# Forget columns moved into the key-rope piece, which comes first of the feature pieces; score products on 128 rows; squares of the second block's A attention one piece ahead of their sums

## What is computed

```python
logf = jax.nn.log_sigmoid((a_f + b_forget[l]).astype(jnp.float32))   # a_f: 6 columns of h @ w_in
cum_logf = jnp.cumsum(logf, axis=1)
a_out = _fox_attention(a_q, a_k, a_v, cum_logf)       # 6 heads of 128; adds cum[q] - cum[k] to the scores
...
q_nope, q_rope = q[..., :B_NOPE], _rope(q[..., B_NOPE:], pos)
k_rope = _rope(b_krope[:, :, None, :], pos)[:, :, 0, :]              # 64 columns, the same for all heads
b_out = _mla_attention(q_nope, q_rope, k_nope, k_rope, b_v)          # 6 heads: 128 + 64 wide
...
c_out = _diff_attention(...)                                         # 4 heads, two scores of 64 each
x = x + jnp.einsum('bsm,md->bsd', mixed, w_out[l])
```

## Time and profile before

| what | value |
|---|---|
| median of 3 runs | 2325.93 us (2325.87 to 2327.4) |
| the profiled execution, its own time | 2325.4 us |
| its span, first to last instruction | 2323.6 us |
| TensorE products (PE) busy | 2164.6 us, 93% |
| VectorE (DVE) busy | 1376.7 us, 59% |
| ScalarE (ACT) busy | 727.5 us, 31% |
| DMA | 761.82 MB, mean 328 GB/s |
| mean granted clock of TensorE | 0.988 |
| the first block ends, about | 972 us |
| the second block's attention ends, about | 1340 us |

### The profile page before, as it was taken

The page is one execution under the profiler, slowest core; times in us unless marked ns, Lnnn a source line. Parts: engine busy times, 40 slices in busy tenths (PEclk is TensorE's granted clock), DMA queues, the critical chain, the costliest instruction groups (busy, mean ns, idle before and its releaser), DMA issues. The chain is left out here.

```text
span 2323.6 us, 35590 instructions
## 1 busy us (share of the span) xinstructions
PE 2164.6 (93%) x14439; PEld 1634.7 (70%) x14439; DVE 1376.7 (59%) x2161; ACT 727.5 (31%) x1317; POOL 37.3 (2%) x62
## 2 busy tenths in 40 slices
PE   7999999999999999899999979998888989888886
PEld 5799999888999998798898755554444444444443
DVE  6778889987787899765565553333333333333334
ACT  5444555545345544566555320000000000000001
POOL 0000000000000000020000000000000000000000
PEclk9999999999999999999999989999999999999998
DMA  9788777888887778664344269999999999999996
GB/s 351 306 325 313 288 264 292 331 331 321 325 309 275 257 291 336 265 248 150 135 146 140 96 282 430 428 431 432 429 430 432 429 430 432 429 430 431 430 429 286
DMA packets 72674, 761.82 MB, mean 328 GB/s; under 512 B 8128, under 2 KB 11248, under 8 KB 13936
## 3 DMA queue, kind: packets, MB, share of 16 engines
q1 hardware_dynamic: 72416, 759.47, 81.4%
q10 hardware_dynamic: 144, 0.79, 0.1%
HBM read 757.27 MB, written 2.96 MB: 327 GB/s over the span
## 5 line engine op out<-in xcount | busy, mean ns | idle before, releaser
L1218 DVE TENSOR_TENSOR s_w_tail<-s_raw,s_w_head 128x1024 fp32r<-128x1024 f32 x292 | 343.8, 1218 | 17.8 <-ACT s_w_head L828 16.7
L1007 PE MATMUL b_ps<-s_h_head,s_w_head 128*128 128x256 f32 x1184 | 341.2, 288 | 0.0
L828 ACT ACTIVATE s_w_head<-s_raw 128x1024 fp32r<-128x1024 f32 x292 | 294.3, 1051 | 144.0 <-DMA s_raw<-in_w 91.0
L1008 PE MATMUL b_ps<-s_h_tail,s_w_head 128*128 128x256 f32 x1184 | 334.8, 283 | 0.0
L1009 PE MATMUL b_ps<-s_h_head,s_w_tail 128*128 128x256 f32 x1184 | 334.7, 283 | 0.0
L1335 DVE CUSTOM_DVE_ANT_0 s_raw<-s_raw,s_c_row 128x2048 f32<-128x2048 f32 x128 | 292.0, 2281 | 3.2 <-DMA s_c_row<-c_row_dram 3.2
L2442 PE MATMUL b_ps<-s_raw,s_window 128*64 128x256 f32 x2048 | 227.6, 380 | 38.7 <-DMA s_raw<-in_w_up 20.7
L2442 PEld LDWEIGHTS b_ps<-s_raw,s_window 128*64 128x64 f32 x2048 | 155.2, 137 | 116.2 <-issue 30.6
L1007 PEld LDWEIGHTS b_ps<-s_h_head,s_w_head 128*128 128x128 f32 x1184 | 226.7, 191 | 5.6 <-issue 5.3
L1008 PEld LDWEIGHTS b_ps<-s_h_tail,s_w_head 128*128 128x128 f32 x1184 | 226.9, 192 | 0.2
L1009 PEld LDWEIGHTS b_ps<-s_h_head,s_w_tail 128*128 128x128 f32 x1184 | 226.7, 191 | 0.0
(11 more groups left out here) (357 smaller groups left out, 3468.4 us busy)
## 6 DMA issues: line engine op xcount, KB each, us to landing
s_raw<-in_w SPq DMA_DIRECT2D x198, 1024.0 KB, 5.5
s_raw<-in_w_ada SPq DMA_DIRECT2D x128, 1024.0 KB, 6.0
s_raw<-in_w_gate SPq DMA_DIRECT2D x16, 4096.0 KB, 32.8
s_raw<-in_w_up SPq DMA_DIRECT2D x16, 4096.0 KB, 30.7
s_raw<-in_w_down SPq DMA_DIRECT2D x32, 2048.0 KB, 26.9
s_down<-in_w_down SPq DMA_DIRECT2D x16, 2048.0 KB, 27.6
s_spare<-in_w_gate SPq DMA_DIRECT2D x8, 4096.0 KB, 32.9
s_down<-in_w_gate SPq DMA_DIRECT2D x8, 4096.0 KB, 32.9
```

Source lines behind the costliest of these rows:

```text
L828: act.activation(w_head[:, g % SPLITS, cols], raw[:, ring, cols], ACT.Copy)\
L1007: pe.matmul(out, head, m_head, start=first, stop=False, skip_group_check=True)
L1008: pe.matmul(out, head, m_tail, start=False, stop=False, skip_group_check=True)
L1218: dve.tensor_tensor(w_tail[:, g % SPLITS, cols], raw[:, slot["w", g], cols], w_head[:, g % SPLITS, cols].bitcast(F32), ALU.subtract)\
```

## The change

Four edits.

1. The `kr` piece is first of the feature pieces. Its 128 columns are now 64 of rope, 6 of the forget gate and 58 of zeros. The step `forget` follows it (on VectorE and ScalarE alone), `cumsum` one piece later. `prepare`, the 48 products of `forget` and `w_f` in the parameters go. All A pieces move one place down; the pieces from `low` on keep theirs.
2. A scores: `ncum` has 128 partitions, zero but for the six; the second product uses 128 rows. B scores: odd heads use a second key tile, `late_key`, whose lower half is zero, even heads `rope[:, 3, :]`, whose upper half is set to zero; both products use 128 rows. GpSimd clears `ncum` and `late_key` once at the start.
3. The first layer's `x_rows` stands behind token piece (1, 3) instead of (1, 1). VectorE's `rel` no longer waits for the running sum; `forget` waits until `rel` has been read out.
4. In the second block `onorm` is two steps: `osq` (the squares on ScalarE) and `onorm` (the rest). For A they are one piece apart, the squares in the old place; for B both stay.

A new entry in `STEP_RANK` names a step that no list holds. The diff, cut:

```diff
-                  ("subln_g", 1), ("lam_init", 1), ("one_minus", 1), ("w_f", 96)):
+                  ("subln_g", 1), ("lam_init", 1), ("one_minus", 1)):
...
+        out[n] = 0.0
+        out[n].reshape(P, KT, P)[:, :, 0:B_ROPE + 6] = wi[:, :, np.concatenate([r(bkr, B_ROPE), r(af, 6)])]
+        n += 1
...
     pieces = [("tok", b, g) for b in range(4) for g in range(4)]
+    pieces += [("feat", "kr", 0)]
     for h in range(6):
         pieces += [("feat", "aq", h), ("feat", "ak", h), ("feat", "ag", h)]
-    pieces += [("feat", "kr", 0), ("low", 0), ("low", 1), ("low", 2), ("lowv", 0)]
+    pieces += [("low", 0), ("low", 1), ("low", 2), ("lowv", 0)]
...
-        if i == 6:
-            out.append((i, ("forget",)))
-        if i == 8:
-            out.append((i, ("cumsum",)))
+        if piece == ("feat", "kr", 0):
+            out += [(i, ("forget",)), (i + 1, ("cumsum",))]
...
-              ("tok", 1, 1): [("x_rows",)],
+              ("tok", 1, 3): [("x_rows",)],
...
-    return repeated_column(ident[0:6, h:h + 1])
+    return repeated_column(ident[:, B_ROPE + h:B_ROPE + h + 1])
...
+        pool.memset(ncum[:, :], 0.0).then_inc(sem["zeroed"], 1)
+        pool.memset(late_key[:, :], 0.0).then_inc(sem["zeroed"], 1)
...
-                elif kind == "forget":
-                    pe.wait_ge(sem["forget_weights"], at("forget_weights", 0, l))
-                    ps = bank_for(pe, s, l)
-                    for k in range(KT):
-                        ins = three(ps[0:6, 0:T], wf_head[:, 6 * k:6 * k + 6], wf_tail[:, 6 * k:6 * k + 6],
-                                    h_head[:, k, :], h_tail[:, k, :], k == 0, k == KT - 1)
-                    ins.then_inc(full_sem(s, l), 1)
...
+                    if j == 3:
+
+                        for matrix, cols in ((swap, slice(0, T)), (ident, slice(T, 2 * T))):
+                            for out in (slice(0, B_ROPE), slice(B_ROPE, P)):
+                                ins = pe.matmul(ps[out, cols], matrix[:, 0:B_ROPE], rope[:, 3, :], start=True,
+                                                stop=True, skip_group_check=True)
...
-                        r = slice(64 * (h % 2), 64 * (h % 2) + 64)
-                        pairs = [(nope_q[:, h, :], nope_k[:, h, :]), (rope[r, h // 2, :], rope[r, 3, :])]
+                        rope_key = late_key[:, :] if h % 2 else rope[:, 3, :]
+                        pairs = [(nope_q[:, h, :], nope_k[:, h, :]), (rope[:, h // 2, :], rope_key)]
...
-                    dve.wait_ge(sem["decay"], at("decay", 0, l))
...
-                    dve.tensor_tensor(f_row(0), ps[0:6, 0:T], rrow[0:6, :], ALU.mult).then_inc(free_sem(s, l), 1)
...
+                    dve.memset(rope[upper, 3, :], 0.0)
+                    dve.tensor_tensor(o_c[:, 0, :], ps[:, 0:T], sin, ALU.mult)
+                    chain.link(dve.tensor_tensor(o_c[:, 1, :], ps[:, T:2 * T], cos, ALU.mult))
+                    dve.tensor_tensor(rope[lower, 3, :], o_c[lower, 0, :], o_c[lower, 1, :], ALU.add)\
+                       .then_inc(free_sem(s, l), 1)
+                    dve.tensor_tensor(late_key[upper, :], o_c[upper, 0, :], o_c[upper, 1, :], ALU.add)\
                        .then_inc(sem["roped"], 1)
...
-                out.append((i + (4 if name == "A" else 3), ("onorm", name)))
+                at = i + (4 if name == "A" else 3)
+                out += [(at, ("osq", name)), (at + (name == "A"), ("onorm", name))]
```

More of the change, by code:

```diff
@@ L170, in first_weights @@
             feats += [r(aq + P * h, P), r(ak + P * h, P), r(ag + P * h, P)]
-        krope = np.concatenate([r(bkr, 64), r(bkr, 64)])
-        for c in feats + [krope]:
+        for c in feats:
             out[n].reshape(P, KT, P)[:] = wi[:, :, c]
@@ L245, in with_followers @@
     return steps
-STEP_RANK = {"score": 1, "gated": 2, "gate": 3, "ada": 8, "soft": 9, "mixed": 10}
+STEP_RANK = {"score": 1, "gated": 2, "gate": 3, "ada_turn": 5, "ada": 8, "soft": 9, "mixed": 10}
 def in_turn(steps):
@@ L342, in layer_schedule @@
         steps = steps[:need] + moved + [last] + [s for s in steps[need:] if s not in moved]
-    return [("prepare",)] + steps
+    return steps
 NEXT_NORM = {("out", 1, 3): [("squares", 0), ("turn_x", 0)],
@@ L439, in psum_plan @@
             take(s, 6)
-        elif kind in ("value", "subnorm", "forget"):
+        elif kind in ("value", "subnorm"):
             take(s, 7)
@@ L638, in f_row @@
     def f_row(n):
-        return nope_k[0:6, n, :]
+        return nope_k[B_ROPE:B_ROPE + 6, n, :]
     def par_of(name, l, lo=0, hi=None):
@@ L1137, in _ @@
                     ps = bank_for(pe, s, l)
-                    pe.matmul(ps[:, 0:T], swap, rope[:, j, :], start=True, stop=True)\
-                        .then_inc(full_sem(s, l), 1)
+                    if j == 3:
[3 more added lines that the diff above has]
+                                                stop=True, skip_group_check=True)
+                        ins.then_inc(full_sem(s, l), 1)
+                    else:
+                        pe.matmul(ps[:, 0:T], swap, rope[:, j, :], start=True, stop=True)\
+                            .then_inc(full_sem(s, l), 1)
                 elif kind == "score":
@@ L1359, in _ @@
                 elif kind == "forget":
-                    ps = full(dve, s, l)
-                    freed(dve, ("x_rows",), l)
-                    if l:
-                        dve.wait_ge(sem["rel_out"], 16)
-                    dve.tensor_tensor(f_row(0), ps[0:6, 0:T], rrow[0:6, :], ALU.mult).then_inc(free_sem(s, l), 1)
-                    freed(dve, s, l)
-                    bias = par_of("b_forget", l)[0:6, :]
-                    dve.tensor_scalar(f_row(1), f_row(0), bias, 0.0, ALU.add, ALU.min)
-                    chain.link(dve.tensor_scalar(f_row(0), f_row(0), bias, None, ALU.add))
+                    dve.wait_ge(sem["rel_out"], 16)
+                    freed(dve, ("feat", "kr", 0), l)
+                    logits = rope[B_ROPE:B_ROPE + 6, 3, :]
+                    bias = par_of("b_forget", l)[B_ROPE:B_ROPE + 6, :]
+                    dve.tensor_scalar(f_row(1), logits, bias, 0.0, ALU.add, ALU.min)
+                    chain.link(dve.tensor_scalar(f_row(0), logits, bias, None, ALU.add))
                     dve.scalar_tensor_tensor(out=f_row(2), in0=f_row(0), scalar=-1.0, in1=f_row(0),
@@ L1375, in _ @@
                     dve.wait_ge(sem["f_abs"], at("f_abs", 0, l))
-                    dve.tensor_tensor_scan(out=ncum[:, :], data0=f_row(4), data1=f_row(1), initial=0.0,
+                    dve.wait_ge(sem["zeroed"], 2)
+                    dve.tensor_tensor_scan(out=ncum[B_ROPE:B_ROPE + 6, :], data0=f_row(4), data1=f_row(1), initial=0.0,
                                            op0=ALU.add, op1=ALU.subtract).then_inc(sem["decay"], 1)
@@ L1382, in _ @@
                     ps = full(dve, s, l)
-                    dve.tensor_tensor(o_c[:, 0, :], ps[:, 0:T], sin, ALU.mult).then_inc(free_sem(s, l), 1)
-                    chain.link(dve.tensor_tensor(o_c[:, 1, :], rope[:, j, :], cos, ALU.mult))
-                    dve.tensor_tensor(rope[:, j, :], o_c[:, 0, :], o_c[:, 1, :], ALU.add)\
+                    if j < 3:
+                        dve.tensor_tensor(o_c[:, 0, :], ps[:, 0:T], sin, ALU.mult).then_inc(free_sem(s, l), 1)
+                        chain.link(dve.tensor_tensor(o_c[:, 1, :], rope[:, j, :], cos, ALU.mult))
+                        dve.tensor_tensor(rope[:, j, :], o_c[:, 0, :], o_c[:, 1, :], ALU.add)\
+                           .then_inc(sem["roped"], 1)
+                        continue
+                    lower, upper = slice(0, B_ROPE), slice(B_ROPE, P)
+                    dve.memset(rope[upper, 3, :], 0.0)
[4 more added lines that the diff above has]
+                    dve.tensor_tensor(late_key[upper, :], o_c[upper, 0, :], o_c[upper, 1, :], ALU.add)\
                        .then_inc(sem["roped"], 1)
@@ L1860, in _ @@
                 act.activation(squares[:, :, :], mixed[:, lo:lo + 8, :], ACT.Square).then_inc(sem["osq"], 1)
+            elif kind == "onorm":
                 ps = full(act, s)
-                if lo:
+                if s[1] == "B":
                     act.wait_ge(sem["onormed"], at("onormed", "A"))
```

25 lines of the change are left out of this document (8 added, 17 removed).

## The result

The changed kernel takes 2291.34 us (2288.75 to 2293.37, four runs), the kernel before 2325.9 on the same chip: a ratio of 0.9851, 95% interval 0.9836 to 0.9867. The forecast was 2290.5. The profiled execution took 2292.39 us for a span of 2290.6, so 33.0 us less span than before.

What follows compares the result with a forecast made beforehand. TensorE, busy 93% of the span, was taken to bound the kernel; 10.96 + 18.8 - 1.4 + 3.8 + 3.0 = 35.2 us off the 2325.4 us profiled execution and 2325.9 median gave 2290.5 us, range 2285.5 to 2297.5.

Steps and rivals of the forecast that it cites:

- The two large terms: TensorE time saved in both layers by dropping the forget products (10.96 us) and by 128-row score products (18.8 us).
- row of norms: First layer's `x_rows` moved two token pieces later: shorter TensorE wait and no half clock, gain 3.8 us (1.2 to 6.4).
- start: Beginning of the run: parameter load shrinks by 98 KB, saving at most 0.2 us.
- Forget columns: 48 six-column products per layer disappear into the k-rope piece: 5.48 us a layer, 10.96 us in all, no cost.
- Scores: A and B heads with all products at 128 rows: 0.785 us for each of 24 heads, 18.8 us.
- Rotation: Rope of the keys, four 64-column products replacing one of 128: cost 0.7 us a layer, bounds 0.43 and 1.5.
- the estimate for the two changes of shape: At the rope of the keys, about 0.1 us for each change of shape on the way in and out.
- I take the middle: First layer's norm products: 3.8 us chosen between no wait left (6.4) and the clock falling once more (1.2).
- The reason I gave for a whole clock: Sums of squares (L2000) ran at full clock after a 2.3 us wait, so the first layer's norm products should too.
- Squares: Second block, squares one piece ahead of sums: waits of 2.3 and 0.7 us go, gain 3.0; late-turn cost bounded at 1.
- Supply: Rival: VectorE and ScalarE become late around the B heads, 9.5 us comes back, 2300 us; chance 0.11.
- the thin lead: Rival: in the 32 output pieces TensorE waits for splits and falls to half clock, 37.6 us, 2328; chance 0.02.

Runs made afterwards that it cites:

- experiment 2: Kernel before, with only the A scores' second product given 128 rows (running sum zero-padded to 128 partitions): 2317.79 us, ratio 0.9966.
- experiment 1: Kernel before, with both short products of each A or B score put behind the long ones: 2316.68 us against 2325.82, ratio 0.9961.
- experiment 8: Repeats: the changed kernel unaltered twice more, 2290.38 and 2292.12 us; the changed kernel with VectorE's diagonal matrices two pieces earlier again, 2289.02 us.
- experiment 7: Changed kernel with VectorE's diagonal matrices made two pieces earlier and the key rotation as two 128-column products: 2289.4 us against 2290.38 on the same chip.

## Why the prediction was right

The forecast missed the median by 0.8 us. The two large terms, 30 of the 35 us, were right in size and in mechanism. That the rest came out so near is in part luck: the medians of the changed kernel alone span 1.7 us, and of the terms below the row of norms is off by 1.3 us and the start by 1.0, both in the same direction, in the first pair of profiles.

- **Forget columns** (said 10.96): 5.48 and 5.51, and 5.60 each when put back. Exact, and VectorE's steps that moved cost TensorE nothing.
- **Scores** (said 18.8): 18.84. The mechanism as well: rows, not the repeated column (experiment 2), and the change between neighbours, not the short product (experiment 1). The forecast's "change of row count" is the right unit; it is 0.19 us a change. The two pages of the Trainium skill then don't contradict each other. The Trainium skill, page TensorE: Matmul & The Clock Gate, section Why this matters for your kernels, has a product with few rows (32 there) take the time of one with 128: the trace of experiment 1 agrees wherever a short product follows another (four short passes start within 0.84 us, 0.65 and one change). The Trainium skill, page TensorEngine Tiling (Array Packing), section Key Properties, has a change of tiling mode drain the engine: the loads of experiment 1 agree (none runs ahead across a change), but the 0.19 us is from the runs alone.
- **Rotation** (said -0.7 a layer): -0.87. The stretch takes 0.87 + 0.43 = 1.30 us, 1.15 said. The two groups of four passes were right (0.49 us, 0.48 said). The step that was off is the estimate for the two changes of shape: 0.1 each, and 1.30 - 0.98 leaves 0.16 each, or 0.22 each if a pair of passes is taken at the 0.216 us at which most of them start. I had spread the B head's 0.79 over eight passes where it belongs to four changes. The bounds held.
- **Row of norms** (said 3.8, ends 1.2 and 6.4): 2.46 in the first pair of profiles. The step that failed there is "I take the middle": the wait was 2.2, 2.6 said, but the clock fell again, 1.2 us for the piece behind and 0.4 for the four products. In two later profiles it did not, and the means of experiment 8 (28.2 and 24.7) give 3.5. The reason I gave for a whole clock, the wait before L2000, does not hold: the same wait of 2.33 us was followed by the half clock in experiments 1 and 2. The wait itself is near by two offsets: the weights landed at 65.14, 64.4 said (two transfers of 5.0 us behind 54.48 are 64.5), and TensorE was through at 66.7, 65.7 said; on time it would have waited over 3 us.
- **Squares** (said 3.0): 3.43. The two waits were 3.0; the rest is in the stretch around them, and no turn came late, which I had bounded with 1 us. Against executions like those of experiments 1 and 2 it is 5.1, a clock fall that the forecast had not priced.
- **Start** (said at most 0.2): 1.01 the other way, in a stretch where TensorE waits for its first transfers. Where TensorE stands there differs by 1 us between profiles of the same program; what sets it in each was not traced. So the sum of terms was 35.2 on paper and 33.0 in this pair of profiles. The later profiles of the changed kernel have spans of 2288.5 and 2288.7, which is 35.1 and 34.9.
- **Supply and the thin lead** (0.11 and 0.02): no wait for a split appears. VectorE still waits 0.57 and 0.56 us for the scores of the last two B heads (0.55 said), but in the first layer no longer for those of the heads before them. The lead of the split over the last B piece fell from 10.95 to 8.67 us; at the thinnest C piece it is unchanged (2.52). The thin lead of the third output piece, which the forecast had called unchanged, is so (1.07 us in the second layer, before and after). What the forecast did not see is another one: VectorE's split of output piece 13 of the second layer ended 1.5 us before TensorE needed it and now ends 0.6 before, 0.3 and 0.5 in the later profiles of the changed kernel and 0.1 in experiment 7. It cost nothing here, but it is what the next gain in front of it will meet.

## What to carry to other kernels

Keep one row count through a run of fp32 products on TensorE: here each change between 128 rows and 6 or 64 cost 0.19 to 0.20 us, so padding an operand with zeros to 128 rows was worth more than the rows it saved; if padding is not possible, put the short products side by side. A handful of weight columns costs as much as 128, so give them a place in a piece that has room. When a step waits for a small tile, move the making of that tile on its own engine, not the step that uses it: moving the whole step gave 3.5 us in the mean of the profiles, moving the tile 1 to 4 more (3.1 by medians) and the same length in all three profiles. And do not price a short wait by its length alone, nor from one profile.

## What I had not expected of the hardware

A change in the number of weight columns from 128 to 6 and back was free (starts 0.12 us apart on both sides), while one from 128 to 64 at the rotation, with its two column halves in use, cost 0.16 to 0.22 us each way. And an idle stretch does not fix what the clock does: after 2.2 us without a product TensorE's clock fell to its half level in one profile, after 2.8 us in the same place of the same program it stayed whole. The same holds at two more places: behind the 2.33 us before the sums of squares it fell in two of four profiles (1.7 us), and between attention and experts, behind stretches of 1.7 and 0.9 us, in four of thirteen (1.3 to 1.5 us).
